# Adding the last four experts' rows to the residual with 0/1 products on chip instead of row scatters to HBM

## The reference, cut to what matters

```python
def first_block(x, ...):
    ...
    x = x + merged @ w_out[l]                       # "the residual" here
    h2 = rmsnorm(x, norm2_g[l])
    x = x + hierarchical_moe(h2, ...)               # sum over experts of
    return x                                        #   c[t,e] * (silu(h2 @ w1[e]) * (h2 @ w3[e])) @ w2[e]

def _layer(x, norm_gain, w_in, ...):                # second block
    xn = _rms(x, norm_gain).astype(x.dtype)
    proj = jnp.einsum('bsd,dp->bsp', xn, w_in)
    ...
    return x + jnp.einsum('bsd,de->bse', merged.astype(x.dtype), w_out)
```

## Time and profile before

| | |
|---|---|
| median of 3 runs | 1455.29 us (1454.27 to 1456.05) |
| profiled execution, its own time | 1457.17 us |
| span of its profile | 1455.4 us |
| PE busy | 1320.5 us (91%) |
| DVE busy | 652.3 us (45%) |
| ACT busy | 494.6 us (34%) |
| POOL busy | 62.5 us (4%) |
| DMA | 205.87 MB, mean 141 GB/s |

### The profile page before, as it was taken

One profiled execution on the slowest core, in us unless ns is written; L12 is line 12 of the kernel. 1 busy time (PEld: TensorE's weight loads), 2 busy tenths in 40 slices (PEclk: granted clock), 3 DMA queues, 4 the chain that ended last, 5 costly groups with the idle time before them and its releaser, 6 DMA issues.

```text
span 1455.4 us, 16711 instructions
## 1 busy us (share of the span) xinstructions
PE 1320.5 (91%) x7003; PEld 1017.3 (70%) x7003; DVE 652.3 (45%) x1077; ACT 494.6 (34%) x768; POOL 62.5 (4%) x71
## 2 busy tenths in 40 slices
PE   6999999999999995888887839999989989799998
PEld 5888887678766784555544438777968866478887
DVE  4354334655466456111111148747566455513253
ACT  4333234456345423111111134444232236422231
POOL 0000000000000000021211100000000001100000
PEclk9999999999999997799999969999999999899999
DMA  6222322112222368899999842101010020112331
GB/s 220 86 87 87 106 70 85 59 58 87 87 87 87 120 270 326 348 402 402 405 405 409 328 130 87 58 1 62 27 33 26 29 87 1 58 59 87 110 122 58
DMA packets 67270, 205.87 MB, mean 141 GB/s; under 512 B 9091, under 2 KB 10229, under 8 KB 54902
## 3 DMA queue, kind: packets, MB, share of 16 engines
q1 hardware_dynamic: 60658, 190.02, 34.8%
q0 software_dynamic: 5824, 12.60, 3.1%
q10 hardware_dynamic: 708, 2.13, 0.4%
HBM read 196.33 MB, written 16.78 MB: 146 GB/s over the span
## 4 chain that ended last, share of the span: by engine, by line
PE 71%; DMA 10%; DVE 9%; ACT 6%; issue 3%; POOL 0%; SPq 0%; POOLq 0%; ACTq 0%; DVEq 0%
PE PS L531 16%; PE PS L533 16%; PE PS L532 16%; PE PS L996 5%; PE PS L528 4%; DMA work<-xn_scratch,slot_tokens 4%; PE PS L850 3%; DMA raw<-in_w 2%; DMA scratch<-in_w 2%; PE PS L878 2%; DVE wlo L1272 2%; ACT work L2143 1%; ACT whi L2143 1%; ACT scratch L2143 1%; PE PS L695 1%
## 5 line engine op out<-in xcount | busy, mean ns | idle before, releaser
L1272 DVE TENSOR_TENSOR wlo<-raw,whi 128x2048 fp32r<-128x2048 f32 x72 | 164.9, 2291 | 281.4 <-ACT whi L2143 281.2
L2143 ACT ACTIVATE whi<-raw 128x2048 fp32r<-128x2048 f32 x72 | 137.6, 1912 | 235.5 <-PE PS L533 220.0
L531 PE MATMUL PS<-whi,hthi 128*128 128x512 f32 x480 | 196.1, 409 | 5.8 <-ACT y_plain L2143 4.1
L531 PE MATMUL PS<-hthi,whi 128*128 128x512 f32 x480 | 198.1, 413 | 0.8 <-DVE htlo L1305 0.8
L2143 ACT ACTIVATE work<-PS 128x512 f32<-128x512 f32 (+3 forms) x150 | 82.6, 563 | 316.6 <-PE PS L878 86.4
L533 PE MATMUL PS<-hthi,wlo 128*128 128x512 f32 x480 | 189.1, 394 | 0.0
L532 PE MATMUL PS<-htlo,whi 128*128 128x512 f32 x480 | 188.7, 393 | 0.0
L533 PE MATMUL PS<-whi,htlo 128*128 128x512 f32 x480 | 188.4, 392 | 0.0
L532 PE MATMUL PS<-wlo,hthi 128*128 128x512 f32 x480 | 188.2, 392 | 0.0
L531 PEld LDWEIGHTS PS<-hthi,whi 128*128 128x128 f32 x480 | 91.3, 190 | 32.8 <-issue 14.2
L528 PE MATMUL PS<-consts,work 128*128 128x128 f32 x456 | 72.1, 305 | 43.2 <-DVE work L1299 24.5
(11 more groups left out here) (345 smaller groups left out, 1812.7 us busy)
## 6 DMA issues: line engine op xcount, KB each, us to landing
raw<-in_w_in SPq DMA_DIRECT2D x44, 1024.0 KB, 5.0
y_plain<-in_w SPq DMA_DIRECT2D x21, 1024.0 KB, 26.1
w_plain<-in_w SPq DMA_DIRECT2D x20, 1024.0 KB, 22.9
h_plain<-in_w SPq DMA_DIRECT2D x20, 1024.0 KB, 25.7
raw<-in_w SPq DMA_DIRECT2D x15, 1024.0 KB, 20.6
merged<-in_w SPq DMA_DIRECT2D x10, 1024.0 KB, 28.1
scratch<-in_w SPq DMA_DIRECT2D x10, 1024.0 KB, 30.2
raw<-in_w_gate SPq DMA_DIRECT2D x8, 1024.0 KB, 5.1
```

What stands on the lines that cost most here:

```text
L531: e.matmul(o, lh, rh, start=start, stop=False)
L1272: tt(lo, raw_place(j), as_f32(hi), SUB).then_inc(*ve.mark("lo", j))
L2143: return e.activation(o, i, f, bias=bias, scale=scale)
```

## The change

The rows of pairs 14 and 15 (`LAST` = 14, the last four experts) are not scattered to HBM. ACT copies both halves rounded to float32r (`rows_hi`), DVE makes the remainder (`rows_lo`), and PE multiplies both by a 0/1 matrix `is_token[n]` (slot x token: 1 where the slot's token is this one) into PSUM, per 128 tokens and 512 columns: 8 groups of 4 products. DVE adds the residual, which SP has loaded from `x2_dram` into `x2_base` (the place of `hthi`) once scatter 13 has landed, and writes the sum to `x1`; SP stores it to `x2_dram` for the end of the kernel. The 0/1 matrices are made by DVE during pair 12, from a row of numbers that POOL counts. The `value_load`s and the splits of units 136 and 137 move, and the squares are written to `xw`.

```diff
+    LAST = PAIRS - 2
+    rows_hi = [w_rounded[:, 1, n, :] for n in range(2)]
+    rows_lo = [w_rounded[:, 0, n, :] for n in range(2)]
+    is_token = [t_rounded[:, 9 + n, :] for n in range(2)]
+    x2_base = h_plain[:, 0:2, :]... "p (i d) -> p i d"
...
 tensor:
         hand_over(PAIRS - 1)
-        down(PAIRS - 1)
         on.wait_ge(*ve["overflow"])
         v = e.value_load(ov_ids[0:1, EXTRA:EXTRA + 1], min_val=0, max_val=EXTRA)
+        down(PAIRS - 1)
+        on.wait_ge(*ve["one-hot"])
+        for i in range(NT):
+            for a in range(2):
+                ps, cols = fresh("x2", i, a), slice(a * BANK, a * BANK + BANK)
+                for n in range(2):
+                    on.wait_ge(*ve["out", "down", LAST + n, a])
+                    tokens = is_token[n][:, i * P:i * P + P]
+                    e.matmul(ps, tokens, rows_hi[n][:, cols], start=n == 0, stop=False)
+                    m = e.matmul(ps, tokens, rows_lo[n][:, cols], start=False, stop=n == 1)
+                m.then_inc(*pe.mark("x2", i, a))
+                bank.filled(("x2", i, a))
         with e.If(v):
...
 vector:
+        def lower_rows(m):
+            on.wait_ge(*pe["bring", m, 1])
+            for a in range(2):
+                cols = slice(a * BANK, a * BANK + BANK)
+                on.wait_ge(*ac["rows hi", m, a])
+                tt(rows_lo[m % 2][:, cols], inside("down", m, a), as_f32(rows_hi[m % 2][:, cols]), SUB).then_inc(
+                    *ve.mark("out", "down", m, a))
         def half_rows(m):
+            if m >= LAST:
+                lower_rows(m)
+                return
...
+            if m == LAST - 2:
+                on.wait_ge(*po["token row"])
+                e.tensor_copy(token_row, token_row_i).then_inc(*ve.mark())
+                e.tensor_copy(last_tokens, idx[:, LAST:PAIRS]).then_inc(*ve.mark())
+                settle()
+                for n in range(2):
+                    ts(is_token[n], token_row, last_tokens[:, n:n + 1], None, ALU.is_equal).then_inc(*ve.mark("one-hot"))
+        v = e.value_load(ov_ids[0:1, EXTRA:EXTRA + 1], min_val=0, max_val=EXTRA)
         half_rows(PAIRS - 1)
-        split()
+        for i in range(NT):
+            on.wait_ge(*x2_tile[i][i])
+            for a in range(2):
+                cols = slice(a * BANK, a * BANK + BANK)
+                on.wait_ge(*pe["x2", i, a])
+                tt(x1[:, i, cols], x2_base[:, i, cols], inside("x2", i, a), ADD).then_inc(*ve.mark("out", "x2", i, a))
         settle()
-        v = e.value_load(...)
         with e.If(v):
...
-        split()
-        normalise("n3", g3)
+        normalise("n3", g3, [split, split])
...
 scalar:
         def half_rows(m):
+            if m >= LAST:
+                for a in range(2):
+                    on.wait_ge(*pe["down", m, a])
+                    act(rows_hi[m % 2][:, a * BANK:a * BANK + BANK], inside("down", m, a), ACT.Copy).then_inc(
+                        *ac.mark("rows hi", m, a))
+                return
...
         hidden(PAIRS - 1)
+        on.wait_ge(*ve["overflow"])
+        v = e.value_load(...)
         half_rows(PAIRS - 1)
         split()
-        (the wait and value_load stood here)
         with e.If(v):
...
-        use(LOGS)
-        split()
-        normalise("n3", g3, lambda i: x2_tile[i][i])
+        normalise("n3", g3, lambda i: ve["out", "x2", i, 1], squares=xw, after=[split])
...
 gpsimd:
+            if m == 0:
+                on.wait_ge(*ve["overflow"])
+                e.iota(token_row_i, pattern=[[1, SEQ]], base=0, channel_multiplier=0).then_inc(*po.mark("token row"))
-            add_rows(m)
+            if m < LAST:
+                add_rows(m)
...
 sync:
+        on.wait_ge(*yo_put[LAST - 1])
+        for s in range(2):
+            on.wait_ge(*pe["unit", raw_in[H_SLOT + s]])
+        for i in range(NT):
+            e.dma_start(x2_base[:, i, :], x2_dram[i * P:i * P + P, :]).then_inc(*x2_tile[i].mark(i))
         on.wait_ge(*ve["overflow"])
         v = e.value_load(...)
+        for i in range(NT):
+            on.wait_ge(*ve["out", "x2", i, 1])
+            e.dma_start(x2_dram[i * P:i * P + P, :], x1[:, i, :]).then_inc(*x2_put.mark())
+        x2_put.also("all")
...
-        on.wait_ge(*yo_put[PAIRS - 1])
-        on.wait_ge(*x1_put["all"])
-        for i in range(NT):
-            e.dma_start(x1[:, i, :], x2_dram[i * P:i * P + P, :]).then_inc(*x2_tile[i].mark(i))
-        on.wait_ge(*x2_tile[NT - 1][NT - 1])
         for j in range(TWO + NR, UNITS):
             load(j)
         on.wait_ge(*pe["stick values", SBH // 2 - 1])
+        on.wait_ge(*x2_put["all"])
         e.dma_start(xw, x2_dram.rearrange("(i p) d -> p i d", p=P)).then_inc(*x2_got.mark("all"))
```

More of the change, by code:

```diff
@@ L164, in build @@
     m_all = sb("merged", [P, KD * SEQ])
+    with nc.sbuf_tensor("w_rounded", [P, 2, 2, 2 * BANK], F32R) as w_rounded:
+        pass
     W = sb("work", [P, 4, UNIT])
+    with nc.sbuf_tensor("t_rounded", [P, 11, BANK], F32R) as t_rounded:
+        pass
     T = sb("scratch", [P, 5632])
@@ L264, in build @@
     ring3 = small(3, 16)
+    last_tokens = small(2)
     info = small(COLS)
@@ L404, in build @@
     ov_pe, ov_ve, ov_ac = (Signal(sem(f"over_{n}")) for n in ("tensor", "vector", "scalar"))
-    ov_xg, ov_w, ov_y = (landing(f"over_{n}") for n in ("tokens", "weights", "rows"))
+    ov_xg, ov_w, ov_y, ov_x2 = (landing(f"over_{n}") for n in ("tokens", "weights", "rows", "residual"))
+    x2_put = landing("x2_stored")
     signals = [pe, ve, ac, po, *x_got, vec_got, row_got, ba_got, ws_got, wr_got, xw_got, g2_got, xn_put, x1_put,
-               x2_got, out_put, *raw_got, *gate_put, *gate_got, *xg_got, yo_put, *x2_tile, ov_pe, ov_ve, ov_ac, ov_xg, ov_w, ov_y]
+               x2_got, out_put, *raw_got, *gate_put, *gate_got, *xg_got, yo_put, *x2_tile, ov_pe, ov_ve, ov_ac, ov_xg, ov_w, ov_y, ov_x2, x2_put]
     bank = Banks()
@@ L459, in build @@
     HT = W[:, 3, 1024:1024 + 4 * P].rearrange("p (u k n) -> p u k n", u=2, k=2)
+    LAST = PAIRS - 2
+    rows_hi = [w_rounded[:, 1, n, :] for n in range(2)]
+    rows_lo = [w_rounded[:, 0, n, :] for n in range(2)]
+    token_row, token_row_i = T[:, 0:SEQ], T[:, 9 * BANK:9 * BANK + SEQ].bitcast(I32)
+    is_token = [t_rounded[:, 9 + n, :] for n in range(2)]
+    x2_base = h_plain[:, 0:2, :].rearrange("p a n -> p (a n)").rearrange("p (i d) -> p i d", i=NT)
     g2_rows = y_plain[:, 1, HB:HB + 2, :].rearrange("p u n -> p (u n)")
@@ L905, in tensor @@
             more.wait_ge(*ac["experts"])
-            more.wait_ge(*yo_put[PAIRS - 1])
+            more.wait_ge(*x2_put["all"])
             for j in range(EXTRA):
@@ L1739, in vector @@
                     half_tokens(m + 1)
-        half_rows(PAIRS - 1)
-        split()
+            if m == LAST - 2:
[6 more added lines that the diff above has]
+        v = e.value_load(ov_ids[0:1, EXTRA:EXTRA + 1], min_val=0, max_val=EXTRA)
+        half_rows(PAIRS - 1)
+        for i in range(NT):
[4 more added lines that the diff above has]
+                tt(x1[:, i, cols], x2_base[:, i, cols], inside("x2", i, a), ADD).then_inc(*ve.mark("out", "x2", i, a))
         ve.also("experts")
         settle()
-        v = e.value_load(ov_ids[0:1, EXTRA:EXTRA + 1], min_val=0, max_val=EXTRA)
         with e.If(v):
@@ L1763, in vector @@
                     e.tensor_copy(oxg[:, cols], OVD[:, half, :]).then_inc(*ov_ve.mark("down", j, half))
-            more.wait_ge(*ov_y[EXTRA - 1])
-        split()
-        normalise("n3", g3)
+            more.wait_ge(*ov_x2["all"])
+        normalise("n3", g3, [split, split])
         on.wait_ge(*po["distance"])
@@ L2161, in root, with normalise @@
             act(y, l, ACT.Exp, scale=-0.5).then_inc(*ac.mark("root", tag))
-        def normalise(tag, gains, ready, before=()):
+        def normalise(tag, gains, ready, before=(), squares=xs, after=()):
             s = tiles(m_all[:, :])
@@ L2167, in normalise @@
                 on.wait_ge(*ready(i))
-                act(xs[:, i, :], s[:, i, :], ACT.Square, accum_out=stat[tag][0][:, i:i + 1]).then_inc(*ac.mark())
+                act(squares[:, i, :], s[:, i, :], ACT.Square, accum_out=stat[tag][0][:, i:i + 1]).then_inc(*ac.mark())
             ac.also("squares", tag)
@@ L2175, in normalise @@
                 *ac.mark(tag, "xs", NT - 1))
+            for a in after:
+                a()
             on.wait_ge(*ve["out", "vectors"])
@@ L2452, in scalar @@
         ac.also("experts")
-        on.wait_ge(*ve["overflow"])
-        v = e.value_load(ov_ids[0:1, EXTRA:EXTRA + 1], min_val=0, max_val=EXTRA)
         with e.If(v):
@@ L2888, in sync @@
             more.wait_ge(*ov_y[EXTRA - 1])
-        on.wait_ge(*yo_put[PAIRS - 1])
-        on.wait_ge(*x1_put["all"])
-        for i in range(NT):
-            e.dma_start(x1[:, i, :], x2_dram[i * P:i * P + P, :]).then_inc(*x2_tile[i].mark(i))
-        on.wait_ge(*x2_tile[NT - 1][NT - 1])
+            for i in range(NT):
```

(3 more changed lines are left out.)

## The result

| | before | changed |
|---|---|---|
| median, first comparison | 1455.64 us (4 runs) | 1444.99 us (1444.47 to 1446.89, 4 runs) |
| ratio, 95% interval | | 0.993 (0.9915 to 0.9945) |
| median, second comparison, another time | 1454.42 us (11 runs) | 1445.57 us (1444.50 to 1446.48, 6 runs) |
| ratio, 95% interval | | 0.9944 (0.9930 to 0.9959) |
| profiled execution, and the span of its profile | 1457.17, 1455.4 us | 1444.63, 1442.9 us |

The change takes 8.9 to 10.7 us off. The prediction was 1444.4 us.

The account below looks back on a forecast made before the run. A seam of latencies (scatters 14 and 15, loads of the sum) was taken as the bound: -11.2 us for these, +0.3 for the residual, 0 for splits, branch and queues, -10.9 in all, giving 1444.4 us; range 1442.5 to 1450.0.

Parts of the forecast that it names:

- The chain of latencies: From last `down` to DVE's statistics, 21.1 us: scatters 14 and 15, loads of the sum, then the last square.
- Products: On PE after `down(15)`: 32 products 0.23 us apart, the last finished at 844.3.
- The small delay of `down(15)`: ACT's second copy of pair 14 precedes the hidden rows' copy, so `down(15)` ends 0.26 us later, at 836.68.
- Last half rows: After `down(15)`: ACT's copy, then DVE's subtraction from PSUM, with the last `rows_lo` ready at 838.14.
- The residual: SP's four loads issued ahead: unit 138 expected by 838.6, tile 0 at about 839.9, costing 0.3 us.
- The first rival: Residual late: loads run only after unit 138 lands at 840.7; 5.6 us of the gain lost, 1449.7 us; chance 0.18.
- the course by the products: PE's products set the pace, DVE's adds one behind: statistics start at 846.35, 11.2 us earlier, before any residual cost.
- The splits: Units 136 and 137 split behind the statistics, beside PE's half-clock turning: cost 0; at full clock splits last, gain 0.2.
- The branch: PE's COMPARE_BRANCH, now behind the 32 products: cost 0, up to 1.5 us kept; as a rival 1445.9 us, chance 0.09.
- the bad case: PE's branch starts only when the last product is done: PE free at 847.9, still 0.5 us of cover.
- The queues: Moved `value_load`s, SP's stores of the sum and units 139 on behind them: cost 0.
- The slower rival: Residual held in SP's queue, its 2 MB taking 21 us to issue: 11.9 us slower, 1467 us; chance 0.03.

Follow-up runs that it names:

- changed_again: The changed kernel, unedited, timed and profiled once more: median 1445.57 us, ratio 0.9944 to the kernel before; seam (last `down` product to second block's first product) 20.96 us.
- residual_first: Changed kernel with SP issuing the four residual tiles ahead of weight units 137 and 138: seam 18.09 us against 19.54; timed again, median 1442.98 us.
- late_split: Changed kernel with DVE's split of unit 137 moved between the fourth and fifth `htlo`: 9.33 us from statistics to first product against 9.25, seam 20.92 us.
- fill: Changed kernel plus 20 unread products on PE behind the 32: turning 3.71 us against 6.28, statistics to first product 8.56 us, seam 18.85 us.
- residual_not_ahead: Changed kernel with SP issuing the residual loads only after pair 15's last `down`: tile 0 landed 5.1 us after issue, seam 20.74 us.

## Why the prediction was right, point by point

**The chain of latencies** at the seam was the right place, and what was saved there reached the end: 588.9 and 588.8 us behind it.

**Products**: 7.6 us from the end of `down` to the end of the last one, as worked out (844.3 - 836.68), 0.23 us apart, at full clock. **The small delay of `down(15)`** was sized at 0.26 and is 0.06: from the start of the turning before it to its first product 1.03 us (830.94 - 829.91), where it was 0.97 (832.77 - 831.80, from the same view of the kernel before); ACT's hidden copy starts at 830.51, 0.11 us before the copy ahead of it ends. **Last half rows**: the last `rows_lo` was ready 1.36 us after `down`, worked out as 1.46.

**The residual** was the term that I was least sure of, and it was too small: 0.3 us. Tile 0 landed 4.0 us after `down` where I had 3.2 and allowed 2.9, and in `changed_again` 5.3. That it would land 1.3 us behind unit 138 was right: 1.25 in both profiles. Unit 138 itself was later against `down` than I had it: it landed at 815.37 + 22.0 = 837.4, 2.8 us after `down`, and 4.1 us after it in `changed_again`, where I had 1.9 (838.6 - 836.68).

The first rival's mechanism was real, and so was its sign: DVE waited for the residual at each tile. What the rival had wrong is the size. It had tile 0 3.2 us behind unit 138 and the others 1.8 us apart; they came 1.25 us apart, and DVE by itself does two adds in 1.2 us, as four adds in a row of the kernel before show:

```profile
1434.74 2.48 DVE L2120 TENSOR_TENSOR work<-PS,work 128x512 f32<-128x512 f32 x4
```

So the waits for the last three tiles cost some 0.05 us each (an estimate from the starts of the adds), and all eight took 5.04 us, where I had 5.5 by multiplying 0.69 by eight: adds in a row overlap. My 837.7 for the moment at which DVE wants tile 0 was also too early by my own sum, since DVE makes the last `rows_lo` until 838.14; the bound of 839.6 does not depend on it. Net against the course by the products (9.54 us, measured in `residual_first`): 0.75 us in one profile, 2.1 in the other.

The Trainium skill ("DMA: Bandwidth & Descriptors", Queues, rings and completion order) has the descriptors of a queue worked off in ring order on each engine, and a completion that lands only after the engine's earlier writes. By that rule tile 0 could not be complete before unit 138 was. These runs agree with it: tile 0 landed 1.25 us behind unit 138, and came in time as soon as it stood ahead of the two units.

**The splits** I costed at 0, since the turning covers them. That was right as long as PE turns from half clock: `late_split` gained nothing. In `fill`, where PE turned at full clock, the splits were last, as the prediction had it for that case, with 8.56 us in place of 8.90. From statistics to first product it is still 9.25 us where I had 8.9, as the turning took 6.28 and 6.56 us against 6.01 before; its length went with the moment at which the clock rose.

**The branch** did not matter in the changed kernel. It took 3.3 us, from 838.0, and PE's queue reached it while the products were still being worked off:

```profile
L925 PEldq COMPARE_BRANCH  x1: 3317/3317/3317, 838.0 to 838.0; - x1
```

Its end at 841.3 is ahead of the last product's at 842.2. I had taken its start at the end of the products as the bad case; it started 4.2 us before it.

**The queues** behind SP's new waits cost nothing, as worked out: ACT's split that takes unit 139 started at 876.71 without a wait, 12.4 us earlier than before. The slower rival needed SP to take 21 us over the residual's issues; it took 4.4.

**The sum**: 10.9 us forecast; by the two profiles, with the 0.06 of `down(15)`, 10.4 and 9.0; by the medians 10.7 and 8.9. The forecast's seam was 9.67 + 0.3 + 8.90 = 18.9 us. Against it the course by the products was 0.1 shorter (9.54), the residual cost 0.75 or 2.1 in place of 0.3, and the way behind the statistics was 0.35 or 0.44 longer: 19.5 and 21.0. So two terms were mis-sized: the residual's, by 0.45 to 1.8 us, and the way from statistics to first product, by 0.35 to 0.44, through the turning. That the first median came within 0.6 us of the forecast is partly luck, for the two measurements of the change are 1.8 us apart.

## What to carry to other kernels

A load that is issued ahead has been brought forward only if its place in the queue has: look at what stands before it in the queue and when that lands, not at when it is issued. Here an issue 8.7 us earlier brought 1.2 us, and moving two loads behind it brought 0.75 to 2.1.

If the last steps of a sum go through a scatter to HBM and back, compare their latency (14 us and more here, with the load) with a few products with a 0/1 matrix (7.6 us for 32) on data that is on chip anyway. How many steps to move follows from what can still land before the last one is computed.

Where removing a limit gains nothing, ask for a second one of the same length beside it, and remove both: 0.7 and 0.0 us alone, 2.3 together.

## What the runs showed of the hardware

COMPARE_BRANCH took between 3.3 us (changed kernel) and 5.7 us (`residual_not_ahead`) on PE over the 14 profiles, 3.6 in the kernel before, and 0.05 on ACT, for a branch over the same kind of skipped block. In the changed kernel it lay beside PE's work; what sets its length isn't shown.

SP's issue of a load is not free behind a backlog in its DMA queue: units 137 and 138 took 8.6 and 10.5 us to issue in the changed kernel and 0.7 us each in `residual_first`, where SP had issued nothing from 808.2 to 825.6 us; the four tiles took 4.40 us behind the units and 1.75 ahead of them.

DVE's adds in a row overlap: those of 0.68 us of the kernel before started 0.60 us apart.

PE's clock was at half when the turning began after 4.8 us of idle PE. With a start at half clock the 32 blocks took 5.2 to 6.6 us, by the moment at which the clock rose; at full clock 3.7. Twenty useless products are cheaper than the idle time that they fill, once DVE's split is out of the way.
